# A four-layer decoder trunk in fp32 on one core: weight splits, means, token sums and first loads issued in another order

## The chip, the cores and the metric

The kernel runs on one core of a Trainium2 chip. The metric is the device time of one launch in microseconds (us), lower is better. The core has five engines with a program each: PE (TensorE, matrix products and transposes), ACT (ScalarE), DVE (VectorE), POOL (GpSimd) and SP, which here only issues transfers. They meet through semaphores. PE reads its operands from the on-chip memory SBUF and writes its results to PSUM. Sixteen DMA engines move data between HBM and SBUF.

## The reference

The input is 256 tokens of width 1024. Four layers follow each other; each is a feed-forward network (FFN) at half weight, an attention, and a second FFN at half weight, each behind an RMS norm and added to x. A last norm ends it.

```python
def rms_norm(x, g):
    y = xf * lax.rsqrt(jnp.mean(xf * xf, axis=-1, keepdims=True) + EPS)
    return (y * g.astype(F32)).astype(x.dtype)

def swiglu(x, w_gate, w_up, w_down):
    return (jax.nn.silu(x @ w_gate) * (x @ w_up)) @ w_down

    for i in range(DEPTH):                      # DEPTH = 4, kind = i % 3
        x = x + 0.5 * swiglu(rms_norm(x, norm_g[i, 0]), ffn_w_gate[i, 0], ffn_w_up[i, 0], ffn_w_down[i, 0])
        h = rms_norm(x, norm_g[i, 1])
        q, k, v = jnp.split(h @ w_qkv[i], 3, axis=-1)
        # kind 0: stick-breaking, 1: differential, 2: forgetting attention -> mix
        x = x + mix @ w_o[i]
        x = x + 0.5 * swiglu(rms_norm(x, norm_g[i, 2]), ffn_w_gate[i, 1], ffn_w_up[i, 1], ffn_w_down[i, 1])
    return rms_norm(x, final_g)
```

The FFN's inner width is 2816. Layers 0 and 3 have stick-breaking attention, layer 1 differential, layer 2 forgetting attention.

## The kernel before

**Products.** Each fp32 product is made of three passes in a narrower format (fp32r). An operand is split in a high part (a rounded copy) and a low part (the value minus the high part); PE makes high by high (L1410), low of the weight by high (L1411) and high of the weight by low (L1412). Every weight comes as a chunk of 1 MB, 128 partitions by 2048 numbers. ACT makes its high part (w_hi, L533), DVE its low part (w_lo, L864). PE can begin a chunk when both are there. `split_to(c)`, in the program of ACT and in that of DVE, is the loop that makes the high or low parts of all chunks up to number c that aren't made yet; so every place where it stands decides what else of that engine comes before or after a split. The high and low parts lie in rings of six slots.

**Chunks.** SP loads the chunks in one fixed list (L452) into a ring of five places, `raw`, and into two more places, SUMS and EXTRA, that the trace calls `extra`. A place is loaded again when the low part (or the sum) made from it is done, which SP waits for, one load after the other. SP's first 20 loads are issued ahead of those of the remaining constants.

**FFN.** Its 22 blocks of inner width are worked through as 11 units. Some are plain: chunks `top` and `bottom` (gate and up), then `down` one unit later. The units 2, 4, 7 and 9 start pairs that are computed with seven products in the place of eight, from sums of weights and sums of tokens. Their chunks: `b11`, `b21`, `b22` as loaded, `t1` (POOL lets a DMA add b12 to b11 in SUMS), and `t3`, `t2`, `t4`, sums that DVE forms (`form`, L876, L880, L884). DVE also makes the four sums of tokens (`early_token_sums` L930, L931; `late_token_sums` L935, L938), and ACT their high parts (`token_sums_hi`). `gated` (L960) multiplies silu(gate), made by ACT (L567), by up. For a unit of a pair, L1020 writes `pair_h`, L1010 and L1004 the sums of its blocks; PE turns the hidden units over (L1602, L1644); ACT and DVE split them (`hidden_hi` L556, `hidden_lo` L924, the trace's m_hi and m_lo).

**Stage borders.** There are 13 norms, n = 0 to 12; the phase behind norm n is an attention for n = 1, 4, 7, 10 and an FFN otherwise. At a border (`next_input`, DVE) the last product of the phase comes out of PSUM bank by bank, four in all. `update` (L1321, or L1317 and `early_update` L1205 behind the differential attention) adds a bank to x; PE transposes it (`turn_part`, L1454, waits for `x_updated`); `gained` (L1327) multiplies by the norm's gain, ACT rounds (`gained_hi` L807) and DVE takes the rest (`gained_lo` L1333, the trace's xg). ACT's `square_sum` (L802), DVE's `norm_mean` (L906) and POOL's power (L497, L498) give 1/rms of each token, `r_col`, which the first silu and `gated` use.

Of the kernel before, what the change touches and what calls it, by code (L numbers as in the profile page):

```python
# [10 lines left out]
ALU = mybir.AluOpType  # L11
# [12 lines left out]
SEVEN = 2, 4, 7, 9  # L24
# [126 lines left out]
def plan():  # L151

    uses, loads, users, places = [], [], [], {}
    for layer, n, c0, att, no in phases():
        order = ATT_ORDER if att else FFN_ORDER
        for w, (what, j) in enumerate(order, c0):
            p = no * len(SEVEN) + SEVEN.index(j) if what in PARTS else None
            if (what, j) == ("down", 0) and n % 3:  # L160
                loads.append(("b11", layer, n % 3, SEVEN[0], SUMS, ("pv", (layer + 1) * PAIRS)))
                loads.append(("b22", layer, n % 3, SEVEN[0], EXTRA, ("pv", (layer + 1) * PAIRS)))
            if (what, j) == ("top", 1) and n == 0:
                loads.append(("b11", 0, 0, SEVEN[0], SUMS, None))
                loads.append(("b22", 0, 0, SEVEN[0], EXTRA, None))
            if what == "t1":
                uses.append((what, no, j, SUMS, p + 1))
            elif what == "b22":
                uses.append((what, no, j, EXTRA, p + 1))
            elif what in FORMS:  # L170
                uses.append((what, no, j, *places[{"t2": "b11", "t3": "b12", "t4": "b21"}[what]]))
            else:
                uses.append((what, no, j, len(users) % RAW, len(users) // RAW + 1))
            for load in ("b12",) if what == "t1" else () if what in (*FORMS, "b22") else (what,):
                r = len(users)
                places[load] = r % RAW, r // RAW + 1
                loads.append((load, layer, n % 3, j, r % RAW, users[r - RAW] if r >= RAW else None))
                users.append(("form", len(FORMS) * (p + 1)) if load == "b11" else
                             ("lo", c0 + order.index(("t4", j)) + 1) if load == "b21" else
                             ("lo", c0 + order.index(("t3", j)) + 1) if load == "b12" else ("lo", w + 1))  # L180
            if n % 3 and layer < DEPTH - 1 and what == "down" and j in (UNITS - 3, UNITS - 2):
                load, place, last = ("b11", SUMS, "t1") if j == UNITS - 3 else ("b22", EXTRA, "b22")
                loads.append((load, layer + 1, 0, SEVEN[0], place, ("lo", c0 + order.index((last, SEVEN[-1])) + 1)))
            if what == "down" and chained(j + 2):
                loads.append(("b22", layer, n % 3, j + 2, EXTRA, ("lo", c0 + order.index(("b22", j)) + 1)))
            if what == "down" and j + 1 in SEVEN[:-1]:
                loads.append(("b11", layer, n % 3, following(j + 1), SUMS, ("lo", c0 + order.index(("t1", j + 1)) + 1)))
            if what == "t4" and j in SEVEN[:-1] and not chained(following(j)):
                loads.append(("b22", layer, n % 3, following(j), EXTRA, ("lo", c0 + order.index(("b22", j)) + 1)))
    return uses, loads  # L190
# [7 lines left out]
def trunk(nc, stream, x_in, gains, consts, lam_in, subln_in, wf_in, bf_in, final_in, out):  # L198
    with ExitStack() as ctx:
# [314 lines left out]
        def _(act):  # L514
# [35 lines left out]
            def ffn(layer, n, c0, _, f):  # L550
# [7 lines left out]

                def token_sums_hi():
                    for i, which in enumerate((S3, S1, S2, S4)):  # L560
                        act.wait_ge(token_sums_ready, BANKS * f + i + 1)
# [28 lines left out]
                def pair_step(s):  # L590
# [40 lines left out]
                    if chained(s):  # L631
# [39 lines left out]
            def attention(layer, n, c0, _, kind):  # L671
# [137 lines left out]
            def next_input(n):  # L809

                if n == 0:
# [7 lines left out]
                    for bank in range(BANKS):  # L819
                        square_sum(0, bank)  # L820
                elif n < NORMS - 1:
                    square_sum(n, 0)
# [4 lines left out]
                    square_sum(n, 3)  # L827
                    gained_hi(n, 2)
                    gained_hi(n, 3)
                else:  # L830
# [19 lines left out]
        def _(dve):  # L850
# [69 lines left out]
            def ffn(layer, n, c0, _, f):  # L920
# [23 lines left out]
                split_to(c0 + 2)  # L944
                if n:
                    norm_mean(n)
# [17 lines left out]
                def plain_step(s):  # L964
                    if s == 0:
                        dve.wait_ge(r_col_ready, n + 1)
                        gated(0, 0)
                        gated(0, 1)
                        if n:
                            early_token_sums()  # L970
                        late_token_sums()
# [13 lines left out]
                    form("t2", q)  # L985
                    split_to(q + 1)
                    gated(s, 0)
# [10 lines left out]
                def pair_steps(s):  # L998
# [60 lines left out]
                    def second_of_chain():  # L1059
# [25 lines left out]
            def attention(layer, n, c0, _, kind):  # L1085
# [113 lines left out]

                def early_update(i):  # L1200
                    if i < BANKS - 1:
                        dve.wait_ge(acc_early, i + 1)
                    else:
                        dve.wait_ge(out_used, (layer + 1) * (PAIRS - 1))
                    nc.vector.tensor_tensor(x_part(i), acc[:, i, :], x_part(i), ALU.add).then_inc(x_early, 1)  # L1205

                def mask(a):
# [48 lines left out]
                for j in range(PAIRS + 1):  # L1256
# [18 lines left out]
                    if j < PAIRS:  # L1275
# [21 lines left out]
                    if j < PAIRS:  # L1297
# [13 lines left out]
            def update(n, i, scale):  # L1311
                bank = banks_of(n)[i]
                dve.wait_ge(acc_ready, BANKS * (n - 1) + i + 1)
                if n == 3 * KINDS.index(DIFF) + 2:
# [5 lines left out]
                    return  # L1320
                nc.vector.scalar_tensor_tensor(out=x_part(bank), in0=acc[:, bank, :], scalar=scale, in1=x_part(bank),  # L1321
                                               op0=ALU.mult, op1=ALU.add).then_inc(x_updated, 1)
# [12 lines left out]

            def next_input(n, scale):

                if n == 0:
                    for half in range(2):
# [6 lines left out]
                        if half == 0:  # L1346
                            first_lo(1)
                    split_to(1)
                elif n < NORMS - 1:
                    update(n, 0, scale)  # L1350
                    update(n, 1, scale)
                    gained(n, 0)
                    update(n, 2, scale)
                    gained(n, 1)
                    gained_lo(n, 0)
                    update(n, 3, scale)
                    gained_lo(n, 1)
                    if n == 3 * KINDS.index(DIFF) + 2:
                        split_to(split[0])
                    gained(n, 2)  # L1360
                    if n % 3 != 1 and n != 3 * KINDS.index(DIFF) + 2:
                        split_to(split[0])
                    gained_lo(n, 2)
                    gained(n, 3)
                    gained_lo(n, 3)
                else:
                    update(n, 0, scale)
                    update(n, 1, scale)
                    final_mean(0)
                    update(n, 2, scale)  # L1370
                    final_output(0, 0)
                    update(n, 3, scale)
                    final_gained()
# [25 lines left out]

            dve.wait_ge(gain_loaded, 16)  # L1400
            next_input(0, 1.0)
            for phase in phases():
                (attention if phase[3] else ffn)(*phase)
                next_input(phase[1] + 1, 1.0 if phase[3] else 0.5)

# [556 lines left out]
```

## Time and profile before

| | |
|---|---|
| median of 3 runs | 1887.27 us (1886.18 to 1889.35) |
| the profiled execution | 1888.41 us, of it 1886.4 us span |
| PE, DVE, ACT busy | 99%, 84%, 60% of the span |
| PE's granted clock over the span | 0.996 of full speed |
| weights and the rest from HBM | 414.74 MB, 220 GB/s over the span |

The profile shows one execution. Its span is what lies between the first and the last instruction, and the device time is 2.0 us more. A share of 99% says that PE is hardly ever idle: what can be won by another order is what is left of idle time on PE, and the stretches in which its clock is lower.

### The profile page before, as it was taken

To read this page: it belongs to the slowest core of one execution; us is meant where nothing else is said; L and a number is where in the kernel's file an instruction comes from. 1 tells how busy PE (TensorE), PEld (TensorE's weight loads), DVE (VectorE), ACT (ScalarE), POOL (GpSimd) and SP (SyncE) were. 2 spreads that over 40 slices of the span, in tenths; PEclk is the share of its full clock that TensorE was granted. 3 is DMA by queue.
4 is the path that set the end of the run, shared out by engine and by line. 5 is a ranking of instruction groups with operands and counts; after the bars stand their busy time and mean duration, and the time that the engine had idled before them with its cause. 6 is when DMAs were issued, how large, how long until landed. Compare 5 with 4: busy or idle time off the path is not lost.

```text
span 1886.4 us, 22668 instructions
## 1 busy us (share of the span) xinstructions
PE 1858.8 (99%) x9268; PEld 1569.5 (83%) x9268; DVE 1581.9 (84%) x1327; ACT 1132.9 (60%) x1156; POOL 66.3 (4%) x75
## 2 busy tenths in 40 slices
PE   9999999999999999999999999999999999999998
PEld 7788898888878899778888888988888788998886
DVE  6989667989898979898899885789899898659897
ACT  5666556656657645566666663466666566556664
POOL 0000000000100000100010000000001000001000
PEclk9999999999999999999999999999999999999999
DMA  7775535776677543577667754467766765527762
GB/s 293 227 299 219 211 135 200 223 264 259 213 244 271 222 177 135 179 224 276 273 198 266 273 209 157 157 209 251 277 264 194 278 223 201 201 107 242 286 236 79
DMA packets 59271, 417.27 MB, mean 221 GB/s; under 512 B 7192, under 2 KB 7456, under 8 KB 8992
## 3 DMA queue, kind: packets, MB, share of 16 engines
q1 hardware_dynamic: 53968, 380.09, 52.0%
q0 software_dynamic: 4608, 33.56, 9.5%
q10 hardware_dynamic: 592, 2.17, 0.3%
q8 instruction: 74, 1.21, 0.3%
q14 instruction: 29, 0.24, 0.0%
HBM read 414.74 MB, written 1.06 MB: 220 GB/s over the span
## 4 chain that ended last, share of the span: by engine, by line
PE 79%; DVE 12%; DMA 5%; issue 2%; ACT 1%; POOL 0%; SPq 0%; POOLq 0%; DVEq 0%; ACTq 0%
PE work L1410 16%; PE work L1412 16%; PE work L1411 16%; PE acc L1410 9%; PE acc L1412 9%; PE acc L1411 9%; DVE w_lo L864 6%; DMA extra<-stream_dram 3%; DMA raw<-stream_dram 1%; DVE raw L880 1%; PE work L1602 1%; PE acc L1454 1%; PE work L1778 1%; ACT w_hi L533 1%; DVE raw L876 1%
## 5 line engine op out<-in xcount | busy, mean ns | idle before, releaser
L864 DVE TENSOR_TENSOR w_lo<-raw,w_hi 128x2048 fp32r<-128x2048 f32 x359 | 810.3, 2283 | 29.4 <-ACT w_hi L533 29.3
L533 ACT ACTIVATE w_hi<-raw 128x2048 fp32r<-128x2048 f32 x359 | 674.4, 1909 | 146.3 <-DVE raw L880 87.2
L1410 PE MATMUL work<-w_hi,xg 128*128 128x512 f32 x880 | 347.5, 395 | 5.0 <-DVE w_lo L864 3.9
L1412 PE MATMUL work<-w_hi,xg 128*128 128x512 f32 x880 | 344.2, 391 | 0.0
L1411 PE MATMUL work<-w_lo,xg 128*128 128x512 f32 x880 | 343.9, 391 | 0.0
L1410 PE MATMUL acc<-w_hi,m_hi 128*128 128x512 f32 x824 | 328.2, 398 | 7.7 <-DVE w_lo L864 7.7
L1412 PE MATMUL acc<-w_hi,m_lo 128*128 128x512 f32 x824 | 321.6, 390 | 0.0
L1411 PE MATMUL acc<-w_lo,m_hi 128*128 128x512 f32 x824 | 320.9, 389 | 0.0
L1412 PE MATMUL work<-w_hi,wide_r 128*128 128x512 f32 x512 | 200.1, 391 | 0.0
L1410 PEld LDWEIGHTS work<-w_hi,xg 128*128 128x128 f32 x880 | 166.0, 189 | 39.7 <-DVE w_lo L864 4.8
L1412 PEld LDWEIGHTS work<-w_hi,xg 128*128 128x128 f32 x880 | 165.9, 189 | 35.1
L1411 PEld LDWEIGHTS work<-w_lo,xg 128*128 128x128 f32 x880 | 166.1, 189 | 33.2
L1410 PEld LDWEIGHTS acc<-w_hi,m_hi 128*128 128x128 f32 x824 | 154.8, 188 | 39.9 <-DVE w_lo L864 10.0
L1412 PEld LDWEIGHTS acc<-w_hi,m_lo 128*128 128x128 f32 x824 | 154.7, 188 | 33.1
L1411 PEld LDWEIGHTS acc<-w_lo,m_hi 128*128 128x128 f32 x824 | 155.0, 188 | 29.9
L1410 PE MATMUL work<-xg,w_hi 128*128 128x256 f32 x512 | 148.8, 291 | 0.2
L864 DVE TENSOR_TENSOR w_lo<-extra,w_hi 128x2048 fp32r<-128x2048 f32 x64 | 146.0, 2282 | 0.0
L1411 PE MATMUL work<-xg,w_hi 128*128 128x256 f32 x512 | 144.8, 283 | 0.0
L1412 PE MATMUL work<-xg,w_lo 128*128 128x256 f32 x512 | 144.8, 283 | 0.0
L533 ACT ACTIVATE w_hi<-extra 128x2048 fp32r<-128x2048 f32 x64 | 122.3, 1912 | 14.6 <-DMA extra<-stream_dram 14.6
L1412 PEld LDWEIGHTS work<-w_hi,wide_r 128*128 128x128 f32 x512 | 96.4, 188 | 20.6
L1410 PE MATMUL work<-w_hi,scratch_r 128*128 128x512 f32 x256 | 103.6, 405 | 0.0
(209 smaller groups left out, 2316.0 us busy)
## 6 DMA issues: line engine op xcount, KB each, us to landing
raw<-stream_dram SPq DMA_DIRECT2D x295, 1024.0 KB, 7.0
extra<-stream_dram SPq DMA_DIRECT2D x64, 1024.0 KB, 4.9
extra<-stream_dram POOLq DMA_DIRECT2D x32, 1024.0 KB, 8.1
x<-x_dram SPq DMA_DIRECT2D x2, 512.0 KB, 7.9
raw<-stream_dram ACTq DMA_DIRECT2D x2, 512.0 KB, 7.6
scratch<-cum_rows ACTq DMA_DIRECT2D x1, 1024.0 KB, 6.7
cst<-consts_dram SPq DMA_DIRECT2D x1, 832.0 KB, 6.6
out_dram<-x SPq DMA_DIRECT2D x3, 256.0 KB, 2.4
```

Of the source, the lines that this page charges most:

```text
L533: nc.scalar.activation(w_hi[:, c % RING, :], raw_at(place), ACT.Copy).then_inc(hi_ready, 1)
L864: nc.vector.tensor_tensor(w_lo[:, c % RING, :], raw_at(place), w_hi[:, c % RING, :].bitcast(F32), ALU.subtract).then_inc(lo_ready, 1)
L876: ins = nc.vector.tensor_tensor(t3, b22, t3, ALU.add)
L880: ins = nc.vector.tensor_tensor(t2, t3, t2, ALU.add)
L1410: nc.tensor.matmul(dst, a_hi, b_hi, start=start, stop=False, skip_group_check=skip)
L1411: nc.tensor.matmul(dst, a_hi, b_lo, start=False, stop=False, skip_group_check=skip)
L1412: return nc.tensor.matmul(dst, a_lo, b_hi, start=False, stop=stop, skip_group_check=skip)
L1454: ins = nc.tensor.transpose(turned(bank)[:, d, :], x_part(bank)[:, d * P:(d + 1) * P], ident)
L1602: ins = nc.tensor.transpose(hidden_bank(s)[:, t * T + tb * P:t * T + (tb + 1) * P], h[:, t * P:(t + 1) * P], ident)
L1778: nc.tensor.matmul(bank, v[:, 0, cols], w[:, 0:T], start=True, stop=True)
```

## The change

PE's and POOL's programs stay as they are, and no operation moves to another engine. What changes is the order of the programs of DVE, ACT and, at the start, SP.

- SP: the first loads of the places SUMS and EXTRA move from behind the second chunk to behind the fifth.
- The end of every FFN that another phase follows (n = 0 to 1, 2 to 3, 3 to 4, 5 to 6, 6 to 7, 8 to 9, 9 to 10): one low part of the next phase goes between the two last `hidden_lo`, and two more go ahead of the first `update`; ACT's high parts go between its `hidden_hi` in the same way.
- Attention to FFN, kinds other than differential (n = 2, 8, 11): one low part ahead of the last m_lo of the attention; then the early token sums, `gated(0, 0)`, the late sums and `gated(0, 1)` in turn.
- FFN to FFN (n = 3, 6, 9): `norm_mean` between the `gained_lo`, and a low part fewer in `next_input`.
- Behind the differential attention (n = 5): `early_update(3)` behind the update of bank 2, a low part ahead of the first update, `norm_mean` ahead of the last `gained_lo`.
- FFN at n = 0: the first unit's silu and gated ahead of the split of `t1`.

```diff
@@ plan @@
-            if (what, j) == ("top", 1) and n == 0:
+            if (what, j) == ("b11", SEVEN[0]) and n == 0:
                 loads.append(("b11", 0, 0, SEVEN[0], SUMS, None))
+            if (what, j) == ("t1", SEVEN[0]) and n == 0:
                 loads.append(("b22", 0, 0, SEVEN[0], EXTRA, None))
@@ scalar, ffn @@
                     if s == 0:
+                        if n:
+                            split_to(c0 + 5)
                         act.wait_ge(r_col_ready, n + 1)
                         silu(0, 0)
+                        if n:
+                            token_sums_hi((0, 1))
                         silu(0, 1)
                         split_to(c0 + 5)
-                        token_sums_hi()
+                        token_sums_hi((2, 3) if n else range(BANKS))
...
-                    split_to(q + 1)
+                    split_to(q + (1 if n else 0))
...
                         if s == UNITS - 2:
+                            split_to(q + 11)
                             hidden_hi(s)
+                            split_to(q + 12)
                             hidden_hi(s + 1)
@@ scalar, attention @@
+                    elif kind != DIFF:
+                        split_to(c0 + ATT_CHUNKS + 1)
...
-                split_to(c0 + ATT_CHUNKS + 2)
+                split_to(c0 + ATT_CHUNKS + (2 if kind == DIFF else 3))
@@ scalar, next_input @@
+                    if n % 3 == 0:
+                        split_to(split[0])
                     gained_hi(n, 3)
@@ vector, ffn @@
                 split_to(c0 + 2)
-                if n:
+                if n % 3 == 2 and layer != KINDS.index(DIFF):
                     norm_mean(n)
...
+                        if n:
+                            early_token_sums()
+                            dve.wait_ge(r_col_ready, n + 1)
+                            gated(0, 0)
+                            late_token_sums()
+                            if n % 3:
+                                gated(0, 1)
+                            split_to(c0 + 5)
+                            if n % 3 == 0:
+                                gated(0, 1)
+                            return
...
                         if s == UNITS - 2:
                             hidden_lo(s)
+                            split_to(q + 11)
                             hidden_lo(s + 1)
+                            split_to(q + 14)
@@ vector, attention @@
+                    if j == PAIRS and kind != DIFF:
+                        split_to(c0 + ATT_CHUNKS + 1)
...
                         apart_mean()
-                        early_update(3)
+                        split_to(c0 + ATT_CHUNKS + 1)
                         dve.wait_ge(r_apart_ready, 1)
...
-                split_to(c0 + ATT_CHUNKS + (0 if kind == DIFF else 1))
+                split_to(c0 + ATT_CHUNKS + (0 if kind == DIFF else 2))
@@ vector, next_input @@
+                elif n == 3 * KINDS.index(DIFF) + 2:
+                    update(n, 0)
+                    update(n, 1)
+                    gained(n, 0)
+                    update(n, 2)
+                    gained_lo(n, 0)
+                    early_update(3)
...
+                    gained(n, 3)
+                    norm_mean(n)
+                    split_to(split[0])
+                    gained_lo(n, 3)
...
-                    if n % 3 != 1 and n != 3 * KINDS.index(DIFF) + 2:
-                        split_to(split[0])
+                    if n % 3 == 0:
+                        norm_mean(n)
                     gained_lo(n, 2)
```

Here is what the programs hold at three places. First SP's program at the start, before: `x` is the input, `raw` a chunk into the ring, `extra` one into SUMS or EXTRA, `cst` a constant.

```order
L456 DMA x<-x_dram 128x2x512
L452 DMA raw<-stream_dram 128x2048
L452 DMA extra<-stream_dram 128x2048 x2
L452 DMA raw<-stream_dram 128x2048
L461 DMA cst<-consts_dram 128x128
L452 DMA raw<-stream_dram 128x2048 x6
L452 DMA extra<-stream_dram 128x2048
```

And with the change:

```order
L457 DMA x<-x_dram 128x2x512
L453 DMA raw<-stream_dram 128x2048 x4
L462 DMA cst<-consts_dram 128x128
L453 DMA extra<-stream_dram 128x2048
L453 DMA raw<-stream_dram 128x2048
L453 DMA extra<-stream_dram 128x2048
L453 DMA raw<-stream_dram 128x2048 x3
```

Four chunks and the constant now stand ahead of the first `extra`, and another chunk ahead of the second.

Second, DVE's program at the end of the first FFN, before:

```order
L864 TENSOR_TENSOR w_lo<-raw,w_hi 128x2048
L1020 SCALAR_TENSOR_TENSOR pair_h<-work,r_col,pair_h 128x256
L864 TENSOR_TENSOR w_lo<-raw,w_hi 128x2048
L924 TENSOR_TENSOR m_lo<-work,m_hi 128x512 x2
L864 TENSOR_TENSOR w_lo<-raw,w_hi 128x2048 x2
L1321 SCALAR_TENSOR_TENSOR x<-acc,x 128x512 x2
L1327 TENSOR_TENSOR wide<-acc,gain 128x512
L1321 SCALAR_TENSOR_TENSOR x<-acc,x 128x512
```

And with the change:

```order
L896 TENSOR_TENSOR w_lo<-raw,w_hi 128x2048
L1061 SCALAR_TENSOR_TENSOR pair_h<-work,r_col,pair_h 128x256
L896 TENSOR_TENSOR w_lo<-raw,w_hi 128x2048
L956 TENSOR_TENSOR m_lo<-work,m_hi 128x512
L896 TENSOR_TENSOR w_lo<-raw,w_hi 128x2048
L956 TENSOR_TENSOR m_lo<-work,m_hi 128x512
L896 TENSOR_TENSOR w_lo<-raw,w_hi 128x2048 x3
L1366 SCALAR_TENSOR_TENSOR x<-acc,x 128x512 x2
L1372 TENSOR_TENSOR wide<-acc,gain 128x512
L1366 SCALAR_TENSOR_TENSOR x<-acc,x 128x512
```

Between the first m_lo and the first x there are two w_lo before and four with the change; one of them has gone between the m_lo. These two w_lo stood further back before, behind the updates.

Third, DVE's program from the attention of layer 0 to the FFN behind it, the part from the mean on, before:

```order
L906 SCALAR_TENSOR_TENSOR mean<-sums 128x2
L864 TENSOR_TENSOR w_lo<-raw,w_hi 128x2048 x2
L960 SCALAR_TENSOR_TENSOR scratch<-work,r_col,scratch 128x256 x2
L930 TENSOR_TENSOR wide<-wide 128x512
L931 TENSOR_TENSOR wide<-wide 128x512
L935 SCALAR_TENSOR_TENSOR wide<-wide 128x512
L938 SCALAR_TENSOR_TENSOR wide<-wide 128x512
```

And with the change:

```order
L938 SCALAR_TENSOR_TENSOR mean<-sums 128x2
L896 TENSOR_TENSOR w_lo<-raw,w_hi 128x2048
L962 TENSOR_TENSOR wide<-wide 128x512
L963 TENSOR_TENSOR wide<-wide 128x512
L992 SCALAR_TENSOR_TENSOR scratch<-work,r_col,scratch 128x256
L967 SCALAR_TENSOR_TENSOR wide<-wide 128x512
L970 SCALAR_TENSOR_TENSOR wide<-wide 128x512
L992 SCALAR_TENSOR_TENSOR scratch<-work,r_col,scratch 128x256
```

The second w_lo behind the mean has gone behind the token sums and the two scratch rows, which are `gated`; the two early sums stand ahead of the first `gated`, and the two late ones between them.

## Rows read from the trace of the kernel before

**Rows 1.** The page: busy time by engine, and the group of low parts.

```profile
PE 1858.8 (99%) x9268; PEld 1569.5 (83%) x9268; DVE 1581.9 (84%) x1327; ACT 1132.9 (60%) x1156; POOL 66.3 (4%) x75
...
L864 DVE TENSOR_TENSOR w_lo<-raw,w_hi 128x2048 fp32r<-128x2048 f32 x359 | 810.3, 2283 | 29.4 <-ACT w_hi L533 29.3
```

**Rows 2.** Waits of PE: engine, line, releaser: us in total, times, longest.

```profile
PE acc L1410 <- DVE w_lo L864: 7.7, 7, 1.4
...
PE work L1602 <- DVE pair_h L1020: 4.7, 2, 2.5
...
PE work L1410 <- DVE w_lo L864: 3.9, 2, 3.0
...
PE work L1410 <- DVE xg L1333: 1.0, 1, 1.0
```

**Rows 3.** Windows of the start: length, busy time, PEclk, DMA share, GB/s.

```profile
10.00:20.00 10.00, 9.76 (x50) 7.78 (x50) 8.91 (x12) 8.00 (x15) 0.40 (x1) 1.00 1.02 420
...
26.00:30.00 4.00, 3.62 (x9) 2.85 (x10) 3.65 (x5) 1.84 (x4) 0.00 (x0) 0.50 0.99 272
...
30.00:34.00 4.00, 4.00 (x14) 3.17 (x13) 3.34 (x3) 1.45 (x1) 0.00 (x0) 0.67 1.01 326
```

**Rows 4.** Timeline of the start: start, length, engine, operation, idle before.

```profile
22.09 1.91 ACT L533 ACTIVATE w_hi<-raw 128x2048 fp32r<-128x2048 f32 x1 [3.22 <-DMA raw<-stream_dram]
...
26.38 0.80 PE L1410 MATMUL work<-w_hi,xg 128*128 128x512 f32 x1 [3.05 <-DVE w_lo L864]
```

**Rows 5.** The chain that ended last, of the start: start, length, what.

```profile
14.58 19.94 DMA raw<-stream_dram
```

**Rows 6.** Timeline of the first pair: DVE's first form, two waits of PE.

```profile
41.10 2.28 DVE L876 TENSOR_TENSOR raw<-extra,raw 128x2048 f32<-128x2048 f32 x1
...
76.72 0.30 PE L1602 MATMUL work<-cst,scratch 128*128 128x128 f32 x1 [2.46 <-DVE pair_h L1020]
...
107.75 0.50 PE L1410 MATMUL work<-w_hi,xg 128*128 128x512 f32 x1 [0.88 <-DVE w_lo L864]
```

**Rows 7.** Timeline of the first FFN's end, DVE and PE.

```profile
186.28 0.69 DVE L924 TENSOR_TENSOR m_lo<-work,m_hi 128x512 fp32r<-128x512 f32 x1 [0.60 <-ACT m_hi L556]
...
188.12 0.69 DVE L924 TENSOR_TENSOR m_lo<-work,m_hi 128x512 fp32r<-128x512 f32 x1 [1.14 <-ACT m_hi L556]
...
189.92 4.49 DVE L864 TENSOR_TENSOR w_lo<-raw,w_hi 128x2048 fp32r<-128x2048 f32 x2 [1.11 <-ACT w_hi L533]
...
194.34 0.69 DVE L1321 SCALAR_TENSOR_TENSOR x<-acc,x 128x512 f32<-128x512 f32 x1
...
195.50 0.60 PE L1454 MATMUL acc<-cst,x 128*128 128x128 f32 x4
```

**Rows 8.** Timeline ahead of the last attention m_lo of layer 0, DVE.

```profile
298.92 0.69 DVE L1161 TENSOR_TENSOR m_lo<-work,m_hi 128x512 fp32r<-128x512 f32 x1 [2.39 <-ACT m_hi L730]
```

**Rows 9.** Chain and timeline of one loop of the second FFN.

```profile
350.39 0.69 DVE L1010 TENSOR_TENSOR scratch<-work,scratch 128x512 f32<-128x512 f32 x1 [0.17 <-PE work L1412]
...
353.30 7.26 DMA extra<-stream_dram
...
360.66 2.29 DVE L876 TENSOR_TENSOR raw<-extra,raw 128x2048 f32<-128x2048 f32 x1 [2.58 <-DMA extra<-stream_dram]
...
371.59 0.50 PE L1410 MATMUL acc<-w_hi,m_hi 128*128 128x512 f32 x1 [1.36 <-DVE w_lo L864]
```

**Rows 10.** DMA queues, 340 to 362 us: packets, MB, share of 16 engines.

```profile
q1 hardware_dynamic: 818, 5.95, 72.0%
...
q0 software_dynamic: 144, 1.05, 25.4%
```

**Rows 11.** Timeline of the border after the differential attention, DVE and PE.

```profile
767.07 0.68 DVE L1205 TENSOR_TENSOR x<-acc,x 128x512 f32<-128x512 f32 x1
...
773.58 0.47 PE L1410 MATMUL work<-w_hi,xg 128*128 128x512 f32 x1 [1.04 <-DVE xg L1333]
...
832.04 0.30 PE L1602 MATMUL work<-cst,scratch 128*128 128x128 f32 x1 [2.26 <-DVE pair_h L1020]
```

More of the change, by code:

```diff
@@ L557, in hidden_hi, with token_sums_hi @@
                                          ACT.Copy).then_inc(h_hi_ready, 1)
-                def token_sums_hi():
-                    for i, which in enumerate((S3, S1, S2, S4)):
+                def token_sums_hi(parts):
+                    for i in parts:
+                        which = (S3, S1, S2, S4)[i]
                         act.wait_ge(token_sums_ready, BANKS * f + i + 1)
@@ L820, in next_input @@
                         square_sum(0, bank)
+                elif n == 3 * KINDS.index(DIFF) + 2:
+                    square_sum(n, 0)
+                    square_sum(n, 1)
+                    gained_hi(n, 0)
+                    square_sum(n, 2)
+                    gained_hi(n, 1)
+                    square_sum(n, 3)
+                    gained_hi(n, 2)
+                    split_to(split[0])
+                    gained_hi(n, 3)
+                elif n % 3 == 2:
+                    square_sum(n, 0)
+                    square_sum(n, 1)
+                    gained_hi(n, 0)
+                    square_sum(n, 2)
+                    gained_hi(n, 1)
+                    square_sum(n, 3)
+                    gained_hi(n, 2)
+                    split_to(split[0])
+                    gained_hi(n, 3)
                 elif n < NORMS - 1:
@@ L828, in next_input @@
                     gained_hi(n, 2)
+                    if n % 3 == 0:
+                        split_to(split[0])
                     gained_hi(n, 3)
@@ L1308, in attention, with early_update, update @@
                         split_to(q_chunk + 5)
-                split_to(c0 + ATT_CHUNKS + (0 if kind == DIFF else 1))
-            def update(n, i, scale):
+                split_to(c0 + ATT_CHUNKS + (0 if kind == DIFF else 2))
+            def early_update(i):
+                if i < BANKS - 1:
+                    dve.wait_ge(acc_early, i + 1)
+                else:
+                    dve.wait_ge(out_used, (KINDS.index(DIFF) + 1) * (PAIRS - 1))
+                nc.vector.tensor_tensor(x_part(i), acc[:, i, :], x_part(i), ALU.add).then_inc(x_early, 1)
+            def update(n, i):
                 bank = banks_of(n)[i]
@@ L1320, in update @@
                     return
-                nc.vector.scalar_tensor_tensor(out=x_part(bank), in0=acc[:, bank, :], scalar=scale, in1=x_part(bank),
+                nc.vector.scalar_tensor_tensor(out=x_part(bank), in0=acc[:, bank, :], scalar=1.0 if n % 3 == 2 else 0.5, in1=x_part(bank),
                                                op0=ALU.mult, op1=ALU.add).then_inc(x_updated, 1)
@@ L1348, in next_input @@
                     split_to(1)
+                elif n == 3 * KINDS.index(DIFF) + 2:
+                    update(n, 0)
[4 more added lines that the diff above has]
+                    early_update(3)
+                    gained(n, 1)
+                    update(n, 3)
+                    gained_lo(n, 1)
+                    gained(n, 2)
+                    gained_lo(n, 2)
+                    gained(n, 3)
+                    norm_mean(n)
+                    split_to(split[0])
+                    gained_lo(n, 3)
                 elif n < NORMS - 1:
-                    update(n, 0, scale)
-                    update(n, 1, scale)
+                    update(n, 0)
+                    update(n, 1)
                     gained(n, 0)
-                    update(n, 2, scale)
+                    update(n, 2)
                     gained(n, 1)
                     gained_lo(n, 0)
-                    update(n, 3, scale)
+                    update(n, 3)
                     gained_lo(n, 1)
-                    if n == 3 * KINDS.index(DIFF) + 2:
+                    gained(n, 2)
+                    if n % 3 == 2:
                         split_to(split[0])
-                    gained(n, 2)
-                    if n % 3 != 1 and n != 3 * KINDS.index(DIFF) + 2:
-                        split_to(split[0])
+                    if n % 3 == 0:
+                        norm_mean(n)
                     gained_lo(n, 2)
```

26 lines of the change are left out of this document (9 added, 17 removed).

## The prediction

> **What bounds the kernel now.** I read the page first. PE is busy in 99% of the span, DVE in 84% [rows 1]. So nothing can be won but PE's idle time and stretches at its lower clock, and the change adds no work to any engine. Second, the table of PE's waits, which says who ends them [rows 2]: 7.7 us in seven waits of L1410 (weights of acc) for a low part, 4.7 in two of L1602 for pair_h, 3.9 in two of L1410 for a low part at the start, 1.0 for xg. That is 17.3 us, all ended by DVE. The reader is to see that each is short: the longest is 3.0 us. Third, windows and timeline of the start, then the chain, to see what DVE itself had waited for: there it is the DMA queue. Last, the timeline at each kind of border, where PE doesn't wait now: what lies between "ready" and "used" there is the slack that a moved low part eats. One low part costs DVE 2283 ns by its group [rows 1]; of four behind each other each takes 2.2 of the chain, since the next begins as the last one drains (two take 4.49 [rows 7], 194.34 − 189.92 = 4.42 from the first start to the next operation).
>
> **The first loads.** ACT stood 3.22 us for the chunk `top` of unit 1, which was high at 24.0, low at 26.3, and PE stood 3.05 [rows 4]. From 10 to 20 us the queues move 420 GB/s at a share above 1 [rows 3]: 1.05 MB take 2.5 us, so two loads fewer ahead of this chunk bring it 5.0 us forward, more than both waits. The 3.05 go. With them goes what follows: between 26 and 30 us the granted clock is 0.50, the lower of its two levels (1.2 of 2.4 GHz), from 30 to 34 it is 0.67, that is 2.6 us at the lower level [rows 3]. 3.6 + 2.6 = 6.2 us at half speed are 3.1 us lost. PE had stood still 3.05 us before its clock fell; without the stand I expect no fall. PE is then 6.1 us ahead at 34 us.
>
> It can't keep all of that. The chunks of the first pair come from the same queue: `b11` lands at 14.58 + 19.94 = 34.52 [rows 5], `b12` one load later, at 37.0, and the same eight loads are ahead of it in both orders. The form t3, which needs it, is at 41.10 [rows 6], so it moves by 4.1 at most. The SUMS place comes later too, and SP's later loads move with DVE's low parts: `t1`'s waits for POOL's add, whose first load now has three more loads ahead of it but meets an emptier queue; I estimate 3.3 for what this leaves of the gain. PE's waits at 76.72 and 107.75 (2.46 and 0.88 [rows 6]) are where this is settled: PE arrives up to 6.1 earlier, DVE 3.3 to 4.1, so the waits grow by the difference and the net is the DVE's. I take the middle: **−3.7**. Bounds: −2.5 (one load) and, if DVE catches up there, −(3.05 + 3.1 + 2.46 + 0.88) = −9.5. The silu and gated of unit 1 ahead of t1's split only exchange two short operations with a low part that waits for POOL's add anyway: 0.
>
> **The seven ends of an FFN.** Two more low parts stand ahead of `update` 0. Before: DVE is at the first m_lo at 186.28, idles 1.14 ahead of the second and 1.11 ahead of two low parts, and is at the update at 194.34 [rows 7]. With the change: m_lo to 186.97 (0.69); low part, 2.2, to 189.17; m_lo, ready since 188.12, some 0.64 until the next can start, to 189.81; three low parts, 6.6, to 196.4. With 0.1 off for overlaps I take 196.30, 1.96 later: 4.4 added, about 2.4 of it in idle time. The update ends at 196.99. PE's transpose ran at 195.50 [rows 7], not before its time: it was ready from 195.03. It will run at 197.04, and PE, which takes its work in order, stands **1.54** where it didn't. Queued behind the update on DVE are the other updates and the gained rows, for which PE waits too; they follow PE's banks, so they move by the same and cost nothing twice. ACT's high parts that go between the m_hi have their chunks in the ring. The same piece stands at seven borders: 7 × 1.54 = **+10.8**. If the other six have more slack than the first, it is less; the nearest bound is 0, if the updates were late by PE's own accumulation, and +13.7 (7 × 1.96) if there were no slack.
>
> **The seven waits in the FFNs (7.7).** They are at the form-driven low parts some 70 us into each FFN behind another phase. One loop shows the pattern: SP issues an `extra` load at 353.30, it lands 7.26 us later, DVE stood 2.58 for it and forms at 360.66, and three operations on PE stands 1.36 at 371.59 [rows 9]. Now DVE comes 2.0 us earlier (n = 2, a low part set into an idle time of 2.39 [rows 8]) up to 3.8 (n = 3, 6, 9, where two low parts are done before the border). DVE stood 0.17 for PE at 350.39, and the low part behind that sum frees the place of this load [rows 9], so its issue hardly moves; but the loads queued ahead of it do, by those 2 to 3.8 us. If its time falls from 7.26 to 6.0, the wait of 1.36 is gone. I take all of it: **−7.7**; the bound on the other side is 0.
>
> A rule of the Trainium skill speaks against this. In the 22 us about this load, POOL's adding DMA has 25.4% of the engines' time beside SP's 72.0% [rows 10], the queues being full together. The Trainium skill, "DMA: Bandwidth & Descriptors", section "Queues, rings and completion order", says that each DMA engine alternates between the queues that have work, a packet at a time. By that rule the loads would slow down as long as the add is under way, whatever their order, the 7.26 would stay and the sum would be 7.7 higher; by the rows' reading it falls. I keep it as a rival.
>
> **Behind differential attention.** `early_update(3)`, 0.68 [rows 11], moves out of the way of the first update, the low part there is exchanged, and PE's wait of 1.04 for xg falls to about 0.2 by the shift of the chain: **−0.8**. PE's wait for pair_h at 832.04, 2.26 [rows 11], is for a DVE that is late, by more low parts than it can hold; two are now ahead of time: **−2.3**. Bounds for both together 0 and −3.3.
>
> **Means, token sums.** Each is done before its user either way; the cover is DVE's low parts, of which PE has at least one in store. 0; uncovered, a low part of 2.2 would be owed once per FFN.
>
> **The sum.** −3.7 + 10.8 − 7.7 − 0.8 − 2.3 = −3.7. The profiled execution took 1888.4, so 1884.7; it lies 1.1 above the median of the runs shown, so **1883.6** against the median. The measurement tells 0.2%, 3.8 us, from no change; the forecast is just at that edge.
>
> **Rivals.**
> *The waits in the FFNs stay* (slower side). The load at 353.30 is issued by a loop that PE bounds and keeps its 7.26. For it: the margin is narrow. Against it: the load ahead moves. It decides from a landing time of 6.0 upward. −3.7 + 7.7 = +4.0: 1891.3. The rule on the queues bears on this one. 0.14.
> *The low parts at the FFN ends cost nothing.* If the updates wait for PE's banks longer than I read, the 10.8 go: −14.5, 1872.8. Against it: 194.34 shows no idle before the update [rows 7], it follows a low part at once. 0.08.
> *DVE catches up in the first pair.* The first term is −9.5 instead of −3.7, and the sum −3.7 − 5.8 = −9.5: 1877.8. For it: DVE was idle in the start too; against it: `b12`'s place in the queue. 0.12.
> *The clock falls behind the new waits.* Seven waits of 1.54, each followed by 2 to 3 us lost as at 26.38 [rows 3, 4]: 7 × 3 = +21 at worst, about half of that if only some do: +10 to +17, up to 1904. Against it: the wait of 1.36 at 371.59 [rows 9] is as long, and the matmul behind it is a full-speed one of 0.50, where that at 26.38 took 0.80. 0.04.
> *The forecast* has 0.62, its own range 1880 to 1887.5.
>
> **How the numbers follow.** The bounds of the terms give the forecast a spread of about ±3.5, so of its 0.62 some 0.33 lie over 0.2% below the median, under 1883.5, the rest within. Faster: 0.32 + 0.08 + 0.12, less a little for what is at the edge = 0.50. Same: 0.29 and a half of the first rival = 0.38. Slower: the rest of it, and the clock = 0.12. The range takes in the first rival short of its end and the third: 1877.5 to 1890.
>
> **What would show it.** The stand of 3.05 at 26 us is gone and no window before 40 us has a clock below 0.9. At the first FFN's end PE waits about 1.5 for the first x, at seven borders, and PE's waits get a row of some 10.8 us for the update's x. The row of acc L1410 behind w_lo falls from 7.7 to about 0. The `extra` load of the second FFN lands within 6 us. The prediction is wrong if PE finds x ready at the borders, or if the low parts wait for the DMA queue elsewhere.

## The result: 0.21% slower

The changed kernel takes 1891.95 us in the median of 20 runs (1887.99 to 1895.53), the kernel before 1887.39 of 20 beside it. The ratio is 1.0021, with a 95% interval of 1.0015 to 1.0028. The forecast was 1883.6, faster by 0.2%, with a range of 1877.5 to 1890.0; the time lies above the range, and it moved the other way. It is where the rival on the slower side stood, "the waits in the FFNs stay", 1891.3, which had a chance of 0.14.

The page of the changed kernel, busy time by engine, and DVE's group of low parts, which answers to [rows 1]:

```profile
PE 1857.3 (98%) x9268; PEld 1567.3 (83%) x9268; DVE 1581.9 (84%) x1327; ACT 1134.9 (60%) x1156; POOL 59.5 (3%) x75
...
L896 DVE TENSOR_TENSOR w_lo<-raw,w_hi 128x2048 fp32r<-128x2048 f32 x359 | 810.3, 2284 | 14.2 <-ACT w_hi L534 14.1
```

The work is the same to the microsecond. DVE's idle time ahead of low parts fell from 29.4 to 14.2, and PE's busy time by 1.5, and still the span is 3.7 longer. How much less DVE waits says nothing about the end, since DVE isn't the engine that bounds the kernel; so the next view is what PE waits for (in total, times, longest), against [rows 2]:

```profile
PE acc L1515 <- DVE x L1366: 9.7, 7, 1.5
PE acc L1471 <- DVE w_lo L896: 6.9, 6, 1.4
PE work L1471 <- DVE w_lo L896: 2.0, 2, 1.1
PE work L1663 <- DVE pair_h L1061: 1.8, 1, 1.8
PE acc L1515 <- DVE x L1362: 1.4, 1, 1.4
```

The first row is new: seven waits for the first x of a border, 9.7 us. The second was 7.7 and was forecast to be about 0. The last is new too: the border behind the differential attention, where the wait for xg (1.0) has gone.

The windows of the start, against [rows 3]:

```profile
10.00:20.00 10.00, 9.76 (x53) 7.88 (x51) 8.86 (x12) 9.16 (x16) 0.00 (x0) 1.00 1.01 420
26.00:30.00 4.00, 4.00 (x21) 3.35 (x20) 3.97 (x6) 2.76 (x4) 0.24 (x1) 1.00 1.03 397
30.00:34.00 4.00, 4.00 (x20) 3.26 (x19) 4.00 (x6) 2.37 (x5) 0.00 (x0) 1.00 1.04 283
```

The granted clock stays at 1.00 where it was 0.50 and 0.67, and PE is busy throughout. The gain isn't all kept. This is DVE's first form, and PE's four waits that follow it in the timeline:

```profile
37.23 2.29 DVE L908 TENSOR_TENSOR raw<-extra,raw 128x2048 f32<-128x2048 f32 x1 [2.57 <-DMA raw<-stream_dram]
...
44.98 0.47 PE L1471 MATMUL work<-w_hi,scratch_r 128*128 128x512 f32 x1 [1.09 <-DVE w_lo L896]
...
72.21 0.30 PE L1663 MATMUL work<-cst,scratch 128*128 128x128 f32 x1 [1.80 <-DVE pair_h L1061]
...
80.31 0.50 PE L1471 MATMUL acc<-w_hi,m_hi 128*128 128x512 f32 x1 [1.37 <-DVE w_lo L896]
...
103.32 0.50 PE L1471 MATMUL work<-w_hi,xg 128*128 128x512 f32 x1 [0.95 <-DVE w_lo L896]
```

The form, at 41.10 before [rows 6], comes at 37.23 and waits for the load of b12, which lands at 37.2 (37.0 before). So DVE is 3.9 us earlier and no more, and PE gives back in these four waits what it is ahead of DVE: they are 5.2 us together, where it had 2.46 and 0.88. (The second of the old waits, 2.46 [rows 6], had brought the clock down once more; the 1.80 didn't.)

The end of the first FFN, DVE and the transpose of PE, against [rows 7]:

```profile
181.92 0.69 DVE L956 TENSOR_TENSOR m_lo<-work,m_hi 128x512 fp32r<-128x512 f32 x1 [0.60 <-ACT m_hi L557]
182.52 2.28 DVE L896 TENSOR_TENSOR w_lo<-raw,w_hi 128x2048 fp32r<-128x2048 f32 x1
184.72 0.69 DVE L956 TENSOR_TENSOR m_lo<-work,m_hi 128x512 fp32r<-128x512 f32 x1
185.32 6.69 DVE L896 TENSOR_TENSOR w_lo<-raw,w_hi 128x2048 fp32r<-128x2048 f32 x3
191.93 1.28 DVE L1366 SCALAR_TENSOR_TENSOR x<-acc,x 128x512 f32<-128x512 f32 x2
...
192.67 0.55 PE L1515 MATMUL acc<-cst,x 128*128 128x128 f32 x3 [1.38 <-DVE x L1366]
```

From the first m_lo to the update it is 10.01 us, where it was 8.06. Read the brackets: the 1.14 and 1.11 of idle time are used, and the low parts don't fit into them.

The same transpose ran at 195.50 before, so PE is 2.83 us ahead behind a wait of 1.38. The last matmul ahead of it starts at 190.90, for 195.27 before: PE came to the border 4.4 ahead and lost 1.5 of it at this wait.

Last, one loop of the second FFN, chain and timeline, against [rows 9]:

```profile
347.64 0.69 DVE L1051 TENSOR_TENSOR scratch<-work,scratch 128x512 f32<-128x512 f32 x1 [0.39 <-PE work L1473]
...
350.56 7.52 DMA extra<-stream_dram
...
358.18 2.29 DVE L908 TENSOR_TENSOR raw<-extra,raw 128x2048 f32<-128x2048 f32 x1 [2.84 <-DMA extra<-stream_dram]
...
369.11 0.50 PE L1471 MATMUL acc<-w_hi,m_hi 128*128 128x512 f32 x1 [1.41 <-DVE w_lo L896]
```

The whole loop stands 2.5 to 2.8 us earlier, as PE does, and has all its waits: DVE waits 0.39 ahead of its sum for 0.17, the load takes 7.52 for 7.26, and PE's wait behind it is 1.41 for 1.36. DVE comes to the loop hardly earlier against PE than before. What it was to gain at the entry of this FFN went before the loop: from the mean up to the sum it stood 1.2 us in all before and stands 3.3 now. Half of that is here, for a high part that ACT could make only when PE had been through:

```profile
322.57 0.60 ACT L557 ACTIVATE m_hi<-work 128x512 fp32r<-128x512 f32 x1 [4.19 <-PE work L1705]
...
323.20 0.69 DVE L956 TENSOR_TENSOR m_lo<-work,m_hi 128x512 fp32r<-128x512 f32 x1 [1.69 <-ACT m_hi L557]
```

### The profile page after: what moved, and what is told of

The parts are those of the page before. It is cut to its first block, busy times and chain, and to the rows that moved or that the text cites. A ratio compares the mean times of both kernels' runs of the same rounds, so it can differ in the third digit from the quotient of the medians.

```text
span 1890.1 us, 22668 instructions
## 1 busy us (share of the span) xinstructions
PE 1857.3 (98%) x9268; PEld 1567.3 (83%) x9268; DVE 1581.9 (84%) x1327; ACT 1134.9 (60%) x1156; POOL 59.5 (3%) x75
## 4 chain that ended last, share of the span: by engine, by line
PE 76%; DVE 15%; DMA 5%; ACT 2%; issue 2%; POOL 0%; SPq 0%; POOLq 0%; DVEq 0%; ACTq 0%
PE work L1471 16%; PE work L1473 16%; PE work L1472 16%; DVE w_lo L896 9%; PE acc L1471 8%; PE acc L1473 8%; PE acc L1472 8%; DMA extra<-stream_dram 3%; DMA raw<-stream_dram 2%; PE acc L1515 1%; PE work L1663 1%; DVE raw L912 1%; DVE m_lo L956 1%; ACT w_hi L534 1%; PE work L1839 1%
## 5 line engine op out<-in xcount | busy, mean ns | idle before, releaser
L896 DVE TENSOR_TENSOR w_lo<-raw,w_hi 128x2048 fp32r<-128x2048 f32 x359 | 810.3, 2284 | 14.2 <-ACT w_hi L534 14.1
```

What stands on the lines that cost most here:

```text
L896: nc.vector.tensor_tensor(w_lo[:, c % RING, :], raw_at(place), w_hi[:, c % RING, :].bitcast(F32), ALU.subtract).then_inc(lo_ready, 1)
```

## The experiments

Ratios are to the kernel before, in runs on the same chip, with 95% intervals. The first four kernels ran on one chip, the last four on another, each four beside the kernel before; so the last four are compared with the kernel with one low part by their ratios. One per thousand is 1.9 us. The rows are of one profiled execution each.

**The start alone**, on the kernel before:

```diff
-            if (what, j) == ("top", 1) and n == 0:
+            if (what, j) == ("b11", SEVEN[0]) and n == 0:
                 loads.append(("b11", 0, 0, SEVEN[0], SUMS, None))
+            if (what, j) == ("t1", SEVEN[0]) and n == 0:
                 loads.append(("b22", 0, 0, SEVEN[0], EXTRA, None))
```

> The kernel before with one part of the change: the first loads of SUMS and EXTRA behind the fifth and sixth chunk. Theory: what the start gives is set by DVE and the load of b12, so 4.2 us are kept of about 6 that PE is ahead at 34 us (the changed kernel is 4.2 ahead just before the first FFN's end): -4.2, about 1883.2, ratio 0.9978. Rival A: DVE catches up in the first pair, -9.5, 1877.9. Rival B: the gain is owed to the other moves in the first FFN, and alone it gives under 2: above 1885.4.

Measured 0.9977 (0.9968 to 0.9985), −4.3 us. The start has its gain by itself, and of the size that the load of b12 leaves. Both rivals are out: −9.5 is outside the interval, and so is less than 2.

**The FFN ends alone**, on the kernel before (ACT's high parts go between the m_hi in the same way, and next_input gives up its low part at n = 3, 6, 9):

```diff
                             hidden_lo(s)
+                            split_to(q + 11)
                             hidden_lo(s + 1)
+                            split_to(q + 14)
```

> The kernel before with another part alone: the high and low parts at the seven FFN ends as in the change (and one low part fewer between the gained rows at FFN to FFN, which the order needs). Theory: each of seven borders puts 1.37 us of standing on PE, +9.6, and the two low parts done early give back at most the 0.9 and 0.3 that the changed kernel's waits at n = 3 and 9 lost: +8.4, about 1895.8, ratio 1.0045. Rival: the low parts in store close the waits in the FFNs behind, 7.7 in all, and the sum is +2 or less: below 1889.4.

Measured 1.0057 (1.0045 to 1.0069), +10.8 us. PE's waits in its profile:

```profile
PE acc L1458 <- DVE x L1325: 10.3, 7, 2.0
PE acc L1414 <- DVE w_lo L866: 7.8, 8, 1.4
PE acc L1414 <- DVE m_lo L926: 4.1, 1, 4.1
```

The low parts in store don't close the waits behind: of the 7.8, 1.4 are in the first FFN, and 6.4 stand for 7.7. The rival is out; the part costs even more than the expected 8.4, though that lies just below the interval. The third row is at the start, which this kernel leaves as it was: PE stood 1.25 at 24.93 and 4.07 at 40.66, where the kernel before stood 3.05 at 26.38. DVE's first form ran at 41.03 for 41.10, and PE came to the first border within 0.3 us of the kernel before. So the waits can lie otherwise in another execution, and DVE sets what the start costs.

One of the seven waits was 1.95, and there the clock fell. The matmuls behind it, from the timeline, and the window about them:

```profile
661.91 0.97 PE L1458 MATMUL acc<-cst,x 128*128 128x128 f32 x4 [1.95 <-DVE x L1325]
...
663.10 0.63 PE L1415 MATMUL acc<-w_lo,m_hi 128*128 128x512 f32 x1
...
666.05 0.40 PE L1415 MATMUL acc<-w_lo,m_hi 128*128 128x512 f32 x1
```

```profile
661.00:665.00 4.00, 3.09 (x10) 2.60 (x11) 2.14 (x4) 1.97 (x5) 0.00 (x0) 0.64 1.01 422
```

By the starts of its matmuls PE lost 3.7 us at this border, for 1.6 at most others: 0.6 of the difference is the longer wait, the rest the clock. So the rival of the clock occurred at one border of this run; in the profiled run of the change, with 1.4 to 1.5 at each, it didn't happen.

**One low part fewer at the FFN ends**, on the changed kernel:

```diff
-                            split_to(q + 14)
+                            split_to(q + 13)
```

> The changed kernel with one low part fewer ahead of the first update at the seven FFN ends: of the two added, only one stays, which fits into the 2.25 us that DVE stood there before. Theory: the 9.6 us of PE's waits for the first x go and nothing else moves: 1891.95 - 9.6 = 1882.3, ratio to before 0.9973. Rival: the low part left out is missing behind the border, PE's waits for low parts rise by as much as the others fall, up to 7 times 2.2: the time stays within 3 us of the change's, above 1889.

Measured 0.9967 (0.9954 to 0.9980), −6.2 us to before and so some 10 to the change. DVE's timeline at the same border, and PE's transpose:

```profile
185.28 4.48 DVE L896 TENSOR_TENSOR w_lo<-raw,w_hi 128x2048 fp32r<-128x2048 f32 x2
189.93 0.69 DVE L1366 SCALAR_TENSOR_TENSOR x<-acc,x 128x512 f32<-128x512 f32 x1 [0.17 <-PE acc L1473]
...
191.10 0.60 PE L1515 MATMUL acc<-cst,x 128*128 128x128 f32 x4
```

The update now waits 0.17 for PE's bank instead of PE for the update. The transpose is at 191.10 for 192.67: the border costs 1.57, of which 1.38 stands in the wait. The other 0.2 is that a wait is counted from the modelled end of the matmul before: the last one ahead of the transpose has 0.40 us in this profile, and the transpose starts 0.24 behind its start. The row of waits in the FFNs is 7.5 for 6.9: the low part left out is hardly missed.

**None of the moves at the FFN ends**, on the changed kernel:

```diff
                             hidden_lo(s)
-                            split_to(q + 11)
                             hidden_lo(s + 1)
-                            split_to(q + 14)
```

> The changed kernel without the moves at the seven FFN ends: two low parts between the last m_lo and the first update as before, the rest of the change kept. Theory: PE's waits for the first x go, as with one low part fewer: -9.6, and the waits at n = 3 and 9 come back by 1.2: 1883.5, ratio 0.9979. Rival: without a store of low parts every FFN waits once more by about a low part, 2.2 in seven: above 1890.

Measured 0.9984 (0.9976 to 0.9993), −3.0 us. PE's waits for low parts in acc are 9.1 us in eight places here, for 7.5 in six. With the kernel of one low part this makes a series: of the two added low parts none gives −3.0, one −6.2, both +4.0. One fits into the idle time and is worth about 3; the second costs 10. A part of what the one is worth is a row that neither that kernel nor the changed one has:

```profile
PE work L1701 <- DVE scratch L990: 2.0, 3, 0.7
```

L990 is `gated` here. PE stands 0.67 for it in the first unit of each FFN behind an FFN (n = 3, 6, 9), where the change put `gated(0, 1)` behind a split; the low part in store covers this. This kernel has the start and all that is left of the change, and with 0.9984 against 0.9977 for the start alone, the moves of means, token sums and attention ends together give nothing that can be measured. That is a sum of gains and costs: the wait for pair_h behind the differential attention, 1.9 us with the start alone, is gone, and these 2.0 have come.

**The load of the loop issued earlier**, on the kernel with one low part:

```diff
                         gate_11()
-                        sum_22()
                         split_to(q + 7)
+                        sum_22()
                         split_to(q + 8)
```

> one_low with one exchange in the first pair of each chain: the low part of b22, which frees the place of the extra load, goes ahead of the sum on which DVE waits for PE. Theory: PE's wait of up to 1.4 in seven FFNs is the load's time above 5.9 us after an issue that PE's pace sets; in one_low DVE is ready some 1.2 to 1.4 us before the sum can run, the load is issued that much earlier, and most of the 7.5 us go: -5, about 1875.5, ratio to before 0.994. Rival: the queue sets the landing, not the issue; the load lands when it did, and the time stays at 1880.5, with the sum 1 us late besides.

Measured 0.9938 (0.9926 to 0.9950), −11.7 us, the fastest kernel of the study. The chain and DVE's timeline in the second FFN, and the waits of PE:

```profile
344.11 2.28 DVE L896 TENSOR_TENSOR w_lo<-extra,w_hi 128x2048 fp32r<-128x2048 f32 x1
346.30 0.68 DVE L1051 TENSOR_TENSOR scratch<-work,scratch 128x512 f32<-128x512 f32 x1
...
353.28 2.29 DVE L908 TENSOR_TENSOR raw<-extra,raw 128x2048 f32<-128x2048 f32 x1 [1.49 <-DMA extra<-stream_dram]
```

```profile
PE acc L1471 <- DVE w_lo L896: 3.3, 5, 1.4
```

DVE's wait ahead of the sum is gone, since the low part fills it; its wait for the load falls from 2.38 to 1.49. PE's row falls from 7.5 to 3.3, with 1.4 in the first FFN in both; the wait for pair_h in the first FFN falls too, from 2.10 to 0.43, and PE comes to the first border 1.4 us further ahead. 1875.7 on the scale of the expectation is what the theory gave, though it hadn't counted this second part. The rival, that the queue alone sets the landing, is out. The seven loads took no less time, 7.1 us in the mean for 6.7: they were issued earlier, at this one by 1.1 us against PE.

**Half of that load left out**, on the kernel with one low part:

```diff
-                sp.dma_start(raw_at(place), stream[i]).then_inc(...)
+                cols = slice(0, 1024 if place == EXTRA and free is not None and free[0] == "lo" else 2048)
+                sp.dma_start(raw_at(place)[:, cols], stream[i][:, cols]).then_inc(...)
```

> one_low with half of the bytes left out of those loads of b22 that wait for a low part (its output isn't the reference's). Theory: the load's own transfer is part of the loop; 0.5 MB less land 1.2 us sooner in each of the seven places, and PE's waits for low parts in the FFNs fall from 7.5 to about 1: 1874, ratio 0.993. Rival: POOL's adding DMA or the loads ahead hold it up; then the landing gains less than 0.5 us and the waits stay above 5: 1879.

Measured 0.9956 (0.9943 to 0.9969), −8.3 us, and the row of waits for low parts is 4.2 us. That is 1879.1 on the scale of the expectation: the time is the rival's, and the waits lie between the two. The interval overlaps that of the kernel with one low part. By the landings in the trace the seven loads took 6.7 us in the mean with all bytes (4.8 to 7.6) and 6.1 at half (5.1 to 7.4), where 0.5 MB at 420 GB/s are 1.2. So the load's own bytes are about half of what I took them for, and the scatter is larger than the difference. That the load issued just ahead of it in the same queue holds the rest is my reading, and no run tried it.

**The low part behind the differential attention taken back**, on the kernel with one low part:

```diff
                         apart_mean()
-                        split_to(c0 + ATT_CHUNKS + 1)
                         dve.wait_ge(r_apart_ready, 1)
```

> one_low with the low part ahead of the first update behind the differential attention taken back to where it was. Theory: PE's wait of 1.5 for the first x there goes, the wait of 1.0 for xg comes back, and the wait for pair_h in the next FFN comes back too, 2.3: +1.8, about 1882.3. Rival: only the 1.5 go: 1879.0.

Measured 0.9969 (0.9957 to 0.9982), the same as with it. The wait of 1.5 for the first x has gone, and one of 1.2 for a low part has come a few microseconds later; the wait for pair_h in the FFN behind, 2.26 at 832.04 in the kernel before, didn't come back. (A wait of 2.26 for pair_h in this profile is in the first FFN, where the kernel with one low part has 2.10.) The time can't tell the two expectations apart; the reason in the first one failed: the wait for pair_h isn't closed by this low part.

**Both edits**: the low part of b22 ahead of the sum, and the one behind the differential attention taken back.

> Both of these edits, the low part of b22 ahead of the sum and the one behind the differential attention taken back. Theory: they add up: -5 + 1.8, 1877.3. Rival: with b22 early DVE has slack behind the border and the pair_h wait stays away: 1874.0.

Measured 0.9948 (0.9937 to 0.9960), 1877.6 on the scale of the expectations. The number is the theory's, its reason isn't: the +1.8 was for a wait for pair_h that comes back, and it stays away here too. The rival, 1874.0, is outside the interval. But the kernel with b22 early alone, 0.9938, isn't told apart from it, so the second edit is worth nothing, or costs a little.

## Why the prediction was wrong

*The start, −3.7.* Right, and for the reason given. PE was 4.4 ahead before the first border, and the start alone gave 4.3. The stand of 3.05, the lower clock, the bound by b12's load at 37.0 (the form ran at 37.23) were as forecast.

*The ends of the FFNs, +10.8.* Right. The step from the rows gave 1.54 each, measured are 1.57 at the first border and a row of 9.7 for seven. That the part alone cost 10.8 too is partly luck: in its profile one border costs 2.1 more than the others, for a longer wait and the clock, and other waits are shorter by about as much.

*The waits in the FFNs, −7.7.* This is the step that failed: "its issue hardly moves; but the loads queued ahead of it do, by those 2 to 3.8 us". The waits are 7.7 before and, less the 1.37 at 80.31 in the first FFN, 5.5 after: −2.2 instead of −7.7. Not even all of the 2.2 is the change's: the kernel with the start alone changes nothing at these places, and its row, counted in the same way, is 6.6. The threshold was right: forecast 6.0, measured 5.9. The place was misread: the low part for which PE stands is the seventh operation of DVE behind the form, not the third. Set beside each other, the loads' times in the chain and PE's waits in the trace of before and after give one line: 6.16 us and 0.26, 6.42 and 0.52, 7.01 and 1.11, then no more than 1.4 (7.52 and 1.41). The wait is the load's time less 5.9, up to 1.4. Here is one in the middle, of the change:

```profile
529.84 6.42 DMA extra<-stream_dram
...
547.28 0.50 PE L1471 MATMUL acc<-w_hi,m_hi 128*128 128x512 f32 x1 [0.52 <-DVE w_lo L896]
```

What I had wrong is that an earlier DVE shortens that time. The load ahead, too, is issued when a low part is done, and both moved nearly together: in the second FFN the load ahead was issued at 346.88 for 349.86, 2.98 earlier, the load itself 2.74 earlier, and PE was 2.7 earlier there as well. DVE's lead from the entry of the FFN had by then been spent on waits for ACT (1.69 and 0.90) and for PE at the sum. What is left is scatter, from 6.16 to 7.61 over the seven loops before and from 4.8 to 7.8 with the change; where it comes from no run shows. The experiment with b22 early shows the half of it that counts: with the issue moved out from behind PE's sum, 1.9 of the 6.1 us behind the first FFN were left, though the loads took no less time. Over all kernels without this edit and with full loads the same count lies between 5.5 and 7.7.

*The rule on the queues.* It stood for the rival that came true, but it is not why. The transfers from 350.56 to 358.08 in the changed kernel, by queue:

```profile
q1 hardware_dynamic: 367, 2.65, 92.2%
q14 instruction: 1, 0.01, 0.3%
```

SP's queue has it alone; POOL's adding DMA had landed at 344.28, before this load was issued. It was so before as well: from 353.30 to 360.56 SP's queue had 96.1% and POOL's nothing. My window of 22 us in [rows 10] was too wide to say who was in the way of a load of 7. The Trainium skill, "DMA: Bandwidth & Descriptors", section "Queues, rings and completion order", has an engine alternate between queues with work. No run here shows what two would do to this load.

*Behind the differential attention, −0.8 and −2.3.* The second came: PE has no wait for pair_h there in the changed kernel. The first had the other sign. I counted the low part ahead of the first update as exchanged, and it stands in the path like those at the FFN ends: a wait of 1.45 for the first x took the place of 1.04 for xg, and behind both PE was 0.65 later, +0.65 for −0.8. Which of the changes closes the wait for pair_h is open: start alone and ends alone keep it (1.9 and 1.7), it stays closed without the moves at the FFN ends, and the low part at this border isn't it. The order of `early_update(3)` and `norm_mean` at this border and the token sums behind it are left.

*Means and token sums, 0.* Not measured by themselves. In the changed kernel PE has no wait for them; without the low parts in store it has three of 0.67, so the cover that the prediction counted on is needed.

*The sum.* PE's program is the same in both kernels, so each matmul of one trace can be set beside the same matmul of the other, and the difference of their starts shows where time is lost. The start gives −4.4, the seven borders +11.4 (1.6 each, 1.7 at n = 6 to 7), the seven waits in the FFNs −2.5, the border behind the differential attention +0.65, pair_h −2.4, and three short waits that are new (0.26, 0.24, 0.15, between 1116 and 1298 us) +1.1. That is +3.9, beside +3.7 between the two spans.

*The chances.* 1891.3 for this case was within 0.7 of the median, which is partly luck: the waits didn't all stay, and what they gave back was lost in the other terms and in the new short waits. It was worth more than 0.14: I gave the step on the queue most of the weight though the one row that bore on it, 0.17 of wait for PE ahead of the sum, spoke for the rival.

## What to carry to other kernels

Work put ahead of an operation on the path is free only up to the idle time that stands there, here one low part of 2.2 in 2.25 us; the second cost 1.57 of its 2.2 us at the first border, what was left of it behind the slack there, and again at each of the seven places. Before you count a wait as closed by an engine that comes earlier, find what issues the transfer it waits for, and whether that is tied to the bound engine: then everything in the loop moves together. To shorten such a loop, take the issue out from behind the wait for the bound engine, as with the low part of b22.

## What the runs showed of the hardware

Near two microseconds of standing, PE's clock may fall or not; the length of the stand alone doesn't decide it. It fell behind stands of 3.05 and 2.46 in the kernel before, of 4.07 and 1.95 in the one with the FFN ends alone, and of 2.26 in the one with the low part behind the differential attention taken back. It stayed behind another 2.26 in the kernel before, 2.13 without the moves at the FFN ends, 2.10 with one low part, 2.02 with the start alone, and behind the 1.80 and all stands of 1.4 of the change. Two windows of 4 us in the kernel before, behind the 2.46 and behind the 2.26, show the two outcomes (the last three columns are PEclk, DMA share and GB/s):

```profile
76.00:80.00 4.00, 3.28 (x11) 2.67 (x12) 4.00 (x5) 1.51 (x3) 0.87 (x1) 0.62 0.11 45
...
832.00:836.00 4.00, 3.96 (x19) 3.30 (x20) 4.00 (x3) 1.51 (x3) 0.86 (x1) 1.00 0.11 45
```

Behind the 2.46 the clock is 0.62 in this window and 0.95 in the next 4 us, which is 1.7 us at full speed lost. So a stand of about 2 us cost its own length, or some 1.7 us more.

A transfer of 1 MB took between 4.8 and 7.8 us from its issue to its landing at the same place of equal loops, with SP's queue the only busy one in the loop looked at. Where no queue had moved anything for over 2 us, at 374.53 in the kernel with one low part, a load of 1 MB took 4.82, and the same load at half its bytes 4.39.
